# Mixture-of-experts stage of a decoder layer: the down product in rounded passes, and merged VectorE and ScalarE operations

## The reference, cut to what matters

```python
def expert_block(args):
    tok, e = args
    xb = xt[tok]
    hb = jax.nn.silu(xb @ w1[e]) * (xb @ w3[e])
    return hb @ w2[e]
...
routed = jnp.zeros_like(xt).at[row_tok].add((yb.reshape(P, D) * row_w[:, None]).astype(xt.dtype))
```

## Time and profile before

| | |
|---|---|
| median of 3 runs | 1925.63 us (1923.64 to 1930.85) |
| profiled execution | span 1924.1 us, its only recorded time |
| TensorE matmul busy | 1746.1 us, 91% of the span |
| VectorE busy | 1410.6 us, 73% |
| ScalarE busy | 1137.8 us, 59% |
| GpSimd busy | 465.8 us, 24% |
| experts' loop | 941.4 us (first transpose of activations) to 1886.1 us (last) |
| data moved | 380.04 MB, 198 GB/s mean |

### The profile page before, as it was taken

How to read it: one execution, slowest core, us unless ns; L and a number is a source line. 1 busy time by engine, 2 the same in 40 slices (tenths; PEclk the granted TensorE clock), 3 DMA queues, 4 the chain that set the end, 5 groups by cost and what they waited for, 6 DMA issues and landing times. The chain is left out here.

```text
span 1924.1 us, 38146 instructions
## 1 busy us (share of the span) xinstructions
PE 1746.1 (91%) x10357; PEld 1353.5 (70%) x10358; DVE 1410.6 (73%) x2642; ACT 1137.8 (59%) x2188; POOL 465.8 (24%) x361
## 2 busy tenths in 40 slices
PE   3998999777599978998699999999999999999994
PEld 2787887555378756776577777777777677777773
DVE  6587651588478756666488888888888788888887
ACT  4411221477466543343477777777777677777776
POOL 0011100000022201336233333332333223333231
PEclk8999999999699978999799999999999999999997
DMA  9267610300200162428789978899888999899975
GB/s 358 82 197 208 199 53 28 130 16 17 93 6 8 33 232 77 111 79 173 243 266 294 298 220 277 252 311 332 266 260 292 315 302 284 259 285 300 316 233 194
DMA packets 132525, 380.04 MB, mean 198 GB/s; under 512 B 27365, under 2 KB 39998, under 8 KB 130380
## 3 DMA queue, kind: packets, MB, share of 16 engines
q1 hardware_dynamic: 97276, 288.36, 43.0%
q0 software_dynamic: 35168, 90.60, 19.5%
HBM read 333.82 MB, written 82.13 MB: 216 GB/s over the span
## 5 line engine op out<-in xcount | busy, mean ns | idle before, releaser
L2470 DVE TENSOR_TENSOR w_low<-w_experts,w_high 128x1024 fp32r<-128x1024 f32 x388 | 457.1, 1219 | 91.6 <-issue 63.4
L2411 ACT CAST w_high<-w_experts 128x1024 fp32r x390 | 390.0, 1049 | 94.8 <-issue 80.4
L2393 POOL DMA_INDIRECT acc<-y_rows,scatter_idx x96 | 185.0, 1927 | 604.8 <-DMA acc<-y_rows,scatter_idx 363.6
L2546 PE MATMUL rbank<-w_high,xT_high 128*128 128x512 f32 x776 | 314.7, 406 | 8.5 <-DVE xT_low L2485 8.5
L2546 PE MATMUL rbank<-w_high,xT_low 128*128 128x512 f32 x776 | 308.4, 397 | 0.0
L2546 PE MATMUL rbank<-w_low,xT_high 128*128 128x512 f32 x776 | 305.6, 394 | 0.0
L2568 PE MATMUL rbank<-w_experts,upper 128*128 x384 | 180.8, 593 | 1.9 <-DVE actT_low L2476 1.9
L2546 PEld LDWEIGHTS rbank<-w_high,xT_high 128*128 128x128 f32 x776 | 147.6, 190 | 40.2 <-DVE xT_low L2485 8.1
L2546 PEld LDWEIGHTS rbank<-w_high,xT_low 128*128 128x128 f32 x776 | 146.8, 189 | 33.4
L2546 PEld LDWEIGHTS rbank<-w_low,xT_high 128*128 128x128 f32 x776 | 147.4, 190 | 31.0
L2377 POOL DMA_INDIRECT gathered<-h,idx x96 | 137.5, 1432 | 44.5 <-issue 27.1
(11 more groups left out here) (445 smaller groups left out, 3611.7 us busy)
## 6 DMA issues: line engine op xcount, KB each, us to landing
w_experts<-in_exp_w SPq DMA_DIRECT2D x384, 512.0 KB
qT<-in_w_ada POOLq DMA_DIRECT2D x16, 1024.0 KB, 6.0
w_raw<-in_w_in SPq DMA_DIRECT2D x24, 512.0 KB, 6.8
w_ada<-in_w_ada SPq DMA_DIRECT2D x16, 512.0 KB, 15.1
p_mixed<-mixed SPq DMA_DIRECT2D x8, 512.0 KB, 8.4
w_out<-in_w_out SPq DMA_DIRECT2D x1, 4096.0 KB, 12.5
x_kept<-x SPq DMA_DIRECT2D x8, 512.0 KB
acc_tile<-acc SPq DMA_DIRECT2D x8, 512.0 KB, 7.1
```

The source lines that it names most:

```text
L2393: pool.indirect_dma_start(dr["acc"], bass.IndirectOffsetOnAxis(ap=sidx[j][:], axis=0), y[j % 2][:], None, bounds_check=S - 1, oob_is_err=F ...
L2411: act.copy(w13_s[par][0][:, which, k], w13[:, bass.ds(w, 1), which, k].squeeze(1)).then_inc(w_high, 1)
L2470: dve.tensor_tensor(w13_s[par][1][:, which, k], w13[:, bass.ds(w, 1), which, k].squeeze(1), w13_s[par][0][:, which, k], ALU.subtract).then ...
L2546: q = pe.matmul(ps_h[:].rearrange("p (a n) -> p a n", a=2), xT[a][:, k, :], w13_s[par][z][:, :, k, :], start=(k == 0 and m == 0), stop=(k ...
```

## The change

- The whole down product is made in rounded passes: both chunks of the activations and of w2 are split (ScalarE L2417, L2421, VectorE L2479, L2484 of the new code), and TensorE runs 12 rounded products of 128x512 for a block (L2564) in place of two plain and six rounded ones. The copy of the first chunk on VectorE is gone.
- Operations are merged: w1 and w3 are split in two pieces of 128x2048, w2 in one of 128x2048 (before, one chunk of it in two of 128x512), the tokens in one of 128x1024, the result is copied in one of 128x1024.
- The products run pass by pass: all high x high, then the two passes with a low part; the waits on the low parts stand ahead of the passes that use them.
- The row weight is copied by ScalarE behind the token copy, no longer by VectorE. The two index copies on VectorE become one.
- ScalarE copies the result of block b-1 behind the operands of the down product of b, no longer at the end of the iteration of b-1.
- The loads of w2 wait for its split, no longer for the down product.
- The memory that GpSimd's transfers use for their descriptors is set to 8192 bytes; tiles in SBUF move accordingly.

```diff
-    w2_low = at("w2_low", [P, 2, BANK], xg01 + 2 * row, F32R)
-    w2_high = [at(f"w2_high{n}", [P, BANK], xg01 + 2 * row + (2 + n) * BANK * 4, F32R) for n in range(2)]
+    w2_s = [keep["w2_high"], at("w2_low", [P, FC, D], xg01 + 2 * row, F32R)]
...
-        act.sem_inc(y_ready, 1)
-
-        def x_copy(n):
+
+        def x_copy(n, j):
             act.wait_ge(x_mm, n + 1)
-            act.copy(xT[0][:, 0:4, :], ps_x[0][:].rearrange("p (k n) -> p k n", k=4))
-            act.copy(xT[0][:, 4:8, :], ps_x[1][:].rearrange("p (k n) -> p k n", k=4)).then_inc(x_copied, 1)
-
-        def split(n, par, pieces):
-            e, w = entry(act, 0, n, E - 1), entry(act, 1, n, SLOTS - 1)
+            act.copy(xT[0][:], k8(ps_x)).then_inc(x_copied, 1)
+            act.copy(wslot[j][:], xg[j][:, bass.ds(expert_of(act, n) + D, 1)]).then_inc(xw_ready, 1)
...
+        def split(n, par, which):
+            e, w = expert_of(act, n), slot_of(act, n)
             act.wait_ge(w13_ready, e + 1)
-            for which, k in pieces:
-                act.copy(w13_s[par][0][:, which, k], w13[:, bass.ds(w, 1), which, k].squeeze(1)).then_inc(w_high, 1)
+            for a in which:
...
         def down_operands(n):
             act.wait_ge(at_mm, n + 1)
-            act.copy(aT_s[0][:], ps_a[1][:, 0:P]).then_inc(aT_high, 1)
-            e, w = entry(act, 0, n, E - 1), entry(act, 1, n, SLOTS - 1)
+            act.copy(aT_s[0][:], ps_a).then_inc(aT_high, 1)
+            e, w = expert_of(act, n), slot_of(act, n)
             act.wait_ge(w2_ready, e + 1)
-            for half in range(2):
-                act.copy(w2_s[half][0], w2[:, bass.ds(w, 1), 1, half * BANK:(half + 1) * BANK].squeeze(1)).then_inc(d_high, 1)
+            act.wait_ge(dn_mm, n + 1)
+            act.copy(w2_s[0][:], w2[:, bass.ds(w, 1)].squeeze(1)).then_inc(d_high, 1)
...
+        def y_copy(n, j):
+            act.wait_ge(y_free, n + 3)
+            act.wait_ge(dn_mm, n + 2)
+            act.copy(y[j % 2][:].rearrange("p (b n) -> p b n", b=2), ps_y).then_inc(y_ready, 1)
...
                     down_operands(b)
-                    split(b + 2, j % 2, PIECES[2:])
+                    y_copy(b - 1, (j + 3) % 4)
+                    split(b + 2, j % 2, range(1, 2))
                     act.wait_ge(act_ready, b + 1)
                     silu(b + 1)
-                    x_copy(b + 2)
-                    split(b + 3, (j + 1) % 2, PIECES[:2])
-                    act.wait_ge(y_free, b + 3)
-                    act.wait_ge(dn_mm, b + 2)
-                    act.copy(y[j % 2][:, 0:BANK], ps_y[0][:])
-                    act.copy(y[j % 2][:, BANK:], ps_y[1][:]).then_inc(y_ready, 1)
+                    x_copy(b + 2, (j + 2) % 4)
+                    split(b + 3, (j + 1) % 2, range(1))
+        y_copy((nb + 3) // 4 * 4 - 1, 3)
...
+        def indices(i, j):
+            dve.wait_ge(y_free, i * 4 + j + 1)
+            dve.tensor_copy(idx[j][:], list_turns[:, j, bass.ds(i, 2)]).then_inc(idx_ready, 1)
+
+        def split_rest(n, par, which):
+            w = slot_of(dve, n)
+            for a in which:
+                dve.wait_ge(w_high, n * 4 + 2 * a + 2)
+                dve.tensor_tensor(w13_s[par][1][:, a], w13[:, bass.ds(w, 1), a].squeeze(1), w13_s[par][0][:, a],
+                                  ALU.subtract).then_inc(w_low, 2)
...
         def down_rest(n):
-            w = entry(dve, 1, n, SLOTS - 1)
-            dve.wait_ge(aT_high, n + 1)
-            dve.tensor_tensor(aT_s[1][:], ps_a[1][:, 0:P], aT_s[0][:], ALU.subtract).then_inc(aT_ready, 1)
-            for half in range(2):
-                dve.wait_ge(d_high, n * 2 + half + 1)
-                dve.tensor_tensor(w2_s[half][1], w2[:, bass.ds(w, 1), 1, half * BANK:(half + 1) * BANK].squeeze(1), w2_s[half][0],
-                                  ALU.subtract).then_inc(d_low, 1)
-
-        def x_rest(n, j):
+            w = slot_of(dve, n)
+            dve.wait_ge(d_high, n + 1)
+            dve.tensor_tensor(w2_s[1][:], w2[:, bass.ds(w, 1)].squeeze(1), w2_s[0][:], ALU.subtract).then_inc(d_low, 1)
+
+        def x_rest(n):
             dve.wait_ge(x_copied, n + 1)
-            dve.tensor_tensor(xT[1][:, 0:4, :], ps_x[0][:].rearrange("p (k n) -> p k n", k=4), xT[0][:, 0:4, :], ALU.subtract)
-            dve.tensor_tensor(xT[1][:, 4:8, :], ps_x[1][:].rearrange("p (k n) -> p k n", k=4), xT[0][:, 4:8, :], ALU.subtract).then_inc(x_low, 1)
-            dve.tensor_copy(wslot[j][:], xg[j][:, bass.ds(entry(dve, 0, n, E - 1) + D, 1)]).then_inc(xw_ready, 1)
+            dve.tensor_tensor(xT[1][:], k8(ps_x), xT[0][:], ALU.subtract).then_inc(x_low, 1)
...
-                    dve.wait_ge(at_mm, b + 1)
-                    dve.wait_ge(dn_mm, b + 1)
-                    dve.tensor_copy(aT[:], ps_a[0][:, 0:P])
-                    dve.wait_ge(y_free, b + 1)
-                    dve.wait_ge(idx_ready, b + 1)
-                    step.then(dve.tensor_copy(sidx[j][:], idx[j][:]))
-                    index(b + 4, j)
-                    split_rest(b + 2, j % 2, (0, 1))
+                    split_rest(b + 2, j % 2, range(1))
+                    act_rest(b)
+                    indices(i, j)
                     down_rest(b)
-                    split_rest(b + 2, j % 2, (2, 3))
+                    split_rest(b + 2, j % 2, range(1, 2))
                     activate(b + 1, (j + 1) % 4)
-                    x_rest(b + 2, (j + 2) % 4)
-                step.restart()
+                    x_rest(b + 2)
...
         def up(n, par):
+            pe.wait_ge(x_copied, n + 1)
+            pe.wait_ge(w_high, n * 4 + 4)
+            up_pass(n, par, 0, 0)
             pe.wait_ge(w_low, n * 4 + 4)
+            up_pass(n, par, 0, 1)
             pe.wait_ge(x_low, n + 1)
+            up_pass(n, par, 1, 0).then_inc(up_mm, 1)
+
+        def up_pass(n, par, a, z):
             for k in range(KC):
-                for m, (a, z) in enumerate(PASSES):
-                    q = pe.matmul(ps_h[:].rearrange("p (a n) -> p a n", a=2), xT[a][:, k, :], w13_s[par][z][:, :, k, :],
-                                  start=(k == 0 and m == 0), stop=(k == KC - 1 and m == 2))
-            q.then_inc(up_mm, 1)
+                q = pe.matmul(ps_h.rearrange("p (a n) -> p a n", a=2), xT[a][:, k, :], w13_s[par][z][:, :, k, :],
+                              start=(k + a + z == 0), stop=(k == KC - 1 and a == 1))
+            return q
+
+        def down(n):
+            pe.wait_ge(y_ready, n + 1)
+            pe.wait_ge(d_high, n + 1)
+            down_pass(0, 0)
+            pe.wait_ge(aT_ready, n + 1)
+            down_pass(1, 0)
+            pe.wait_ge(d_low, n + 1)
+            down_pass(0, 1).then_inc(dn_mm, 1)
+
+        def down_pass(a, z):
+            for half in range(2):
+                for k in range(FC):
+                    q = pe.matmul(ps_y[:, half, :], aT_s[a][:, k, :], w2_s[z][:, k, half * BANK:(half + 1) * BANK],
+                                  start=(k + a + z == 0), stop=(k == FC - 1 and z == 1))
+            return q
...
+        pe.wait_ge(idx_ready, 4)
...
-                sp.wait_ge(dn_mm, sp.value_load(tab[0:1, 2, bass.ds(after, 1)], min_val=1, max_val=BLOCKS) + 1)
+                sp.wait_ge(d_low, sp.value_load(tab[0:1, bass.ds(after + ENDS, 1)], min_val=1, max_val=BLOCKS))
...
-                    pool.indirect_dma_start(dr["acc"], bass.IndirectOffsetOnAxis(ap=sidx[j][:], axis=0), y[j % 2][:], None,
+                    pool.indirect_dma_start(dr["acc"], bass.IndirectOffsetOnAxis(ap=idx[j][:, 0:1], axis=0), y[j % 2][:], None,
...
-    nc = bacc.Bacc("TRN2", target_bir_lowering=False, num_devices=1)
+    nc = bacc.Bacc("TRN2", target_bir_lowering=False, num_devices=1, dynamic_dma_scratch_size=8192)
```

124 lines of the change are left out of this document (60 added, 64 removed).

## The result

The changed kernel takes **1937.45 us** (median of 14 runs, 1927.94 to 1956.31), the kernel before 1925.83 us (14 runs beside it, 1916.27 to 1930.85). The ratio is 1.0073, with an interval of 1.0054 to 1.0091: slower by some 14 us (the medians are 11.6 apart), where 13 us faster was forecast, and above the forecast range. The profiled execution has a span of 1933.4 us. First its page: the span, the busy times, and the costliest groups of VectorE, ScalarE and GpSimd.

What follows compares the result with a forecast made beforehand. TensorE was taken to pace the experts' loop. Terms of -32 - 6 + 19 + 4 + 2 = -13 us on a span of 1924.1 gave 1911, forecast as 1913 us with the median's 1.5 us offset; its own range was 1903 to 1921.

Steps and rivals of the forecast that it cites:

- TensorE's shorter down product: In the experts' loop, 12 rounded products take 2.76 us, 0.34 less a block; 32 us saved over 95 steps.
- Waits for the tokens' low part: TensorE's 11 waits for the tokens' low part go, as it is used 3.7 us later; 6 us saved.
- Durations of the merged operations: For pieces of 128x2048, a ScalarE copy takes 1.92 us and a VectorE subtraction 2.22 us.
- The feeding chain with its slack of 0.2 us: ScalarE through VectorE to TensorE's transposes: 18.55 of 18.74 us in two blocks; slow register loads lose 19 us.
- Descriptor memory at nothing: Halving the descriptor memory of GpSimd's transfers costs nothing if few transfers are under way.
- a wait of its own is hidden until the scatter chain is the bound: GpSimd is busy 317 of 945 us in the loop, so its own waits cost nothing until scatters bound it.
- The third rival: Scatter chain becomes the bound through the result copy's place ahead of ScalarE's second half and silu; 1935 to 1945, chance 0.13.
- the rival's sign: ScalarE's result copy stands idle before the second half by tens of us.
- Its point of decision: The scatter chain decides once landings take over 10 us for more than some five blocks on end.
- The first, TensorE as only pace: Register loads are rarely slow where it matters, the 19 us loss falls to 0 to 6; 1893 to 1900, chance 0.27.
- The second: Merged pieces starve TensorE in nearly every block; product waits over 35 us, 40 to 48 lost, 1928 to 1936, chance 0.16.
- the 6 us of smaller terms: Weights needed sooner in a faster loop lose 4 us; the later last-but-one result copy loses 2 us.

Runs made afterwards that it cites:

- e10: Changed kernel with VectorE's weight subtractions and ScalarE's copies of w1 and w3 both in pieces of 1024; 1914.53 us, ratio 0.9950 to the kernel before.
- e1: Changed kernel with VectorE's weight subtractions in pieces of 1024, ScalarE's copies left whole; 1919.18 us, ratio 0.9957 to the kernel before.
- e3: Kernel before with descriptor memory halved to 8192 bytes and the freed memory unused; 1927.14 us, ratio 1.0008.
- e7: Kernel before with scatters that write instead of adding; 1909.13 us, ratio 0.9915.
- e4: Changed kernel with the result copy back at the end of its own iteration; 1935.77 us, ratio 1.0057 to the kernel before.
- e6: Changed kernel with scatters that write instead of adding; 1898.44 us, ratio 0.9867 to the kernel before.
- e9: e6 with 840 KB memory-to-memory copies on SyncE's queue, 60 times, replacing the bytes accumulation read; 1898.99 us, ratio 0.9839 to the kernel before.

## Why the prediction was wrong, step by step

- **TensorE's shorter down product: right.** Its shortest blocks are 9.40 to 9.43 us, for 9.37 forecast. The 12 products take 2.85 us (1226.02 to 1228.87), for 2.76: the first four 1.01, the other eight 0.92 for each four, 0.23 apiece.

```profile
1226.02 1.17 PE L2564 MATMUL rbank<-w_high,actT_high 128*128 128x512 f32 x4
1227.03 1.08 PE L2564 MATMUL rbank<-w_high,actT_low 128*128 128x512 f32 x4
1227.95 1.09 PE L2564 MATMUL rbank<-w_low,actT_high 128*128 128x512 f32 x4
1228.87 0.41 PE L2578 MATMUL rbank<-ident,act 128*128 128x128 f32 x2
```

- **Waits for the tokens' low part: right**, none are left.
- **Durations of the merged operations: right.** ScalarE's is 1.91 us (1.92 forecast); VectorE's is 2.29 from the row, 2.27 from start to next start (1213.43 to 1215.70), for 2.22.
- **The feeding chain with its slack of 0.2 us: right in place, and small.** These rows of ScalarE, after the change, answer to the earlier trace rows:

```profile
1216.76 1.01 ACT L2406 CAST xT_high<-rbank 128x1024 fp32r<-128x1024 f32 x1 [0.94 <-PE rbank L2534]
1217.67 0.19 ACT L2407 COPY slot_w<-gathered 128x1 f32 x1
1218.86 1.91 ACT L2413 CAST w_high<-w_experts 128x2048 fp32r x1 [1.00 <-issue]
```

  From the token copy to the half are 2.10 us, for 8.9 less 6.81, 2.09, forecast. TensorE's waits for the product, forecast at 10 to 25 us, are 22.2 on weight loads (4.0 before). e10 takes most of such waits away from e1, which shows that ScalarE's undivided halves made them. The typical block got 0.21 us shorter, where the products alone were to save 0.34: some 12 us of 95 blocks are lost again there, for 19 in my sum.
- **Descriptor memory at nothing: right** (e3).
- **The step that failed: "a wait of its own is hidden until the scatter chain is the bound".** By this step the chain got no term in my sum. I took it as fixed, 9.3 us from two starts in the earlier trace rows, and as nearly, not yet, the bound. Both were wrong. The 9.3 us are not even the chain's: the row of 1224.10 reads "4.95 <-issue", and the trace has the landing before it at 1221.49, so that scatter waited for its result and not for a landing. Over the 73 steps before the change in which the landing came last, issue, landing and restart are 1.91 + 7.28 + 0.90, 10.1 us, above the block. The block that I read, 9.71 us, is the shortest of 95; the median is 9.83. So the chain was already the bound in part: without accumulation the kernel before is 16 us faster (e7), though TensorE looked without a hole at the place I read. And a change on VectorE lengthens it. One cycle is the issue, the landing and the restart: after the change 2.29 + 7.02 + 0.86, 10.17 us, the means over the 92 of 95 steps in which the landing came last, read off the times at which GpSimd's wait ended, against a TensorE block of 9.4. I had the rows for it: in the earlier trace rows one scatter took 2.01 and the next 2.14, the least in that trace is 1.59, and the earlier trace rows shows the subtractions beside them. I never asked why one instruction with one shape had many durations.
- **The third rival had the right direction and the right time, 1935 to 1945, but its mechanism was right in part only.** The chain did become the bound, and the rival's sign came: ScalarE's result copy stood idle for 23.3 us in all. Its point of decision came roughly: a landing took over 10 us behind the end of its issue only once, but 57 of 95 steps from scatter to scatter are over 10 us, in five places for five to eight on end. The rival took its price from the result copy's new place in ScalarE's queue, which e4 excludes, and not from the issue. That it names the measured time is so far luck.
- **First and second rivals.** The first, TensorE as only pace at 1893 to 1900, is out. e6 lies in its range (1898), but only by luck: it leaves the accumulation out, and TensorE still waits 35 us for the product there. The second is out by its own sign: TensorE's waits for the product are 22 us, not over 35, and whole copies on ScalarE remain in e1, which is 18 us faster. Its time, 1928 to 1936, leaves out the 6 us of smaller terms that the forecast and the first rival carry; with them it is 1934 to 1942 and would have held the measured time, again for a wrong reason.

In sums: without the accumulation, the change brings -10.7 us (e6 less e7). As it stands it brings +11.6 by the medians. The difference, 22 us, is what the accumulating scatters take from it, and e1 shows that the length of VectorE's subtractions is worth 18 us, whatever else they do.

**What stays open.** Why a landing takes 7 us, and over 9 in a burst, isn't settled: e9 excludes the sheer bytes for plain scatters, and no run changed the rows of an accumulating one. Nor is it settled why the lateness comes in bursts, and not in every block. Three result buffers, or a weight subtraction with an operand in PSUM, weren't tried.

## What to carry to other kernels

Where an engine issues transfers one by one, add up issue, landing and restart, and hold that cycle against the block before shortening the block: a chain with a few tenths of slack is the next bound. Take its length from many steps in which the landing came last, not from two starts. Leaving one step of it out (here the accumulation) tells its price in one run. Fewer and larger VectorE operations with both inputs in SBUF are not free beside GpSimd: each is a time in which a gather or scatter can't begin its work, so merge the operations that read PSUM, and keep the others as short as VectorE's own load allows. An instruction of one shape with several durations is worth a question before a change is priced. And look at the spread of the blocks beside their mean: here the typical block got faster and the mean slower.
